# All low parts of the weights made on VectorE: 27 halves move from GpSimd's queue to VectorE's

## The chip, the cores and the metric

The kernel runs on one core of a Trainium2 chip. The metric is the device time of one execution in microseconds (us), taken as the median over the runs. Engines: TensorE (PE, with its weight loads PEld), VectorE (DVE), ScalarE (ACT), GpSimd (POOL), and SyncE (SP), which issues most of the DMA transfers.

## The reference

Two transformer blocks on 256 tokens of width 1024, in float32. The first block ends in a layer of product-key experts, and this is the part around the change:

```python
q = (hb @ w_query).reshape(t, PEER_HEADS, 2, PEER_HALF)
s = jnp.einsum('thpc,hpnc->thpn', q, sub_keys).astype(jnp.float32)
v1, i1 = lax.top_k(s[:, :, 0], PEER_TOPK)
v2, i2 = lax.top_k(s[:, :, 1], PEER_TOPK)
cand = (v1[..., :, None] + v2[..., None, :]).reshape(t, PEER_HEADS, PEER_TOPK * PEER_TOPK)
...
best, pos = lax.top_k(cand, PEER_TOPK)
experts = jnp.take_along_axis(cand_idx, pos, axis=-1)
gate = jax.nn.softmax(best, axis=-1).astype(hb.dtype)
...
act = jax.nn.gelu(jnp.einsum('thkd,td->thk', u, hb), approximate=False)
return jnp.einsum('thk,thkd->td', gate * act, vsel)
```

There are 8 heads with two key sets of 128 keys each, 16384 experts, and 16 chosen per head and token. Before it stand the modulation, retention and attention; behind it the second block's two gated feed-forward layers, a state-space mixer and a final projection.

## The kernel before

**Weights.** All weights come in chunks of 128 x 2048 float32 (1 MB) through three raw buffers (`NRAW`). A chunk is two halves of 128 x 1024. Half u belongs to chunk u // 2. Each half is split in two: ScalarE copies it to `w_hi` in the matmul's reduced float32 format (`ahead` in `scalar_program`, line 1608), and `w_lo` = raw - `w_hi` is made by VectorE (`ahead`, line 2118) or, for the halves in `LO_POOL` (line 131), by GpSimd (`ahead`, line 2893; its results are listed at line 2903). There are four buffers of each (`NH`), so the high part of a half waits until TensorE has used the half four before it. `ahead(u)` makes the parts up to half u+3 (`AHEAD`, `REACH`). TensorE computes a half of the expert layer in `feat_half` (line 1297): 16 products with the high part, then a wait for the low part, then 8 products with the low part; then it signals `s_used`. SP loads a chunk when both lows of the chunk three before it are made (line 902, `read`).

**Order.** Each engine's queue is written out by hand, in program order.

**Queries, halves 48 to 63** (`U_QUERY` = 48). For c = 0 to 7, TensorE computes halves 48+2c and 49+2c, then the key scores of c-1 (`key_scores`, line 1334); behind the last two halves it makes those of 6 and 7 one behind the other. ScalarE makes the high parts, copies the queries out of PSUM when both halves of c are used, and then the scores of c-1. VectorE (lines 2513 to 2519) makes lows up to 48+2c+4, waits for the scores of c, and takes the best 16 of four tables (`top16`: max, index, replace).

**Experts, halves 64 to 135 in this stretch** (`U_PEER` = 64). TensorE goes on with one half after another and ScalarE applies `gelu` to each pair. VectorE meanwhile chooses the experts, for each of two blocks of 128 tokens (line 2560): `candidates` adds the score pairs and takes the best 16 of 256 for 8 heads; `chosen(i, 0)` and `chosen(i, 1)` turn positions into indices; between them it reduces `gsel`, for which ScalarE first applies `Exp`. ScalarE does that `Exp` behind the `gelu` of chunk 5 (halves 74 and 75) and of chunk 12 (halves 88 and 89). Between these steps `keep_up` and `ahead` make low parts: up to 70 ahead of the first block's long `top16`, up to 75 behind it, up to 83 ahead of the second block's, up to 88 behind it, and up to 96 at the end. TensorE turns the choice behind half 93 (`turn_choice`), VectorE copies it and makes one-hot tables, and from there TensorE mixes one-hot products (`g_block`) with the halves.

**GpSimd** makes the lows of its 27 halves: 52 to 68, 71 to 75 and 84 to 88. Ahead of 71 and of 84 it waits until VectorE has made the low just before. Behind that it has only a few small instructions and transfers.

The lines of VectorE's queue around the queries:

```python
            for c in range(8):
                for m in range(2):
                    ahead(U_QUERY + 2 * c + m)
                v.wait_ge(s_kse, 2 * c + 2)
                top16([(v16[i][:, hp, :], ix[i][:, hp, :], Ss[i][:, hp, :])
                       for i in range(2) for hp in (2 * c, 2 * c + 1)])
```

Of the kernel before, what the change touches and what calls it, by code (L numbers as in the profile page):

```python
# [84 lines left out]
U_FRONT, U_OUT1, U_QUERY, U_PEER = 0, 40, 48, 64  # L85
# [37 lines left out]
def ffn_at(base, c):  # L123
# [4 lines left out]

LO_POOL = (set(range(U_QUERY + 4, U_PEER + 5)) | set(range(U_PEER + 7, U_PEER + 12))
           | set(range(U_PEER + 20, U_PEER + 25)))

# [272 lines left out]
def program(nc, wall, keys_d, cols_d, rows_d, bigrows_d, crow_d, wmod_d, dist_d, x_d, ctx_d, pT_d, gws_d, out_d, n_chunks):  # L408
    assert n_chunks * 2 == U_END
    with ExitStack() as es:  # L410
# [142 lines left out]
        def lows(u):  # L553
            pool = sum(1 for w in LO_POOL if w <= u)
            return (s_lop, pool) if u in LO_POOL else (s_lov, ORD[u] + 1 - pool)

# [1528 lines left out]
        def vector_program(e):  # L2085
# [32 lines left out]
            def ahead(u, only=False, late=0):  # L2118

                nonlocal made  # L2120
                while made < (ORD[u] + 1 if only else REACH[u] - late):
                    w = SPLIT[made]
                    if w not in LO_POOL:
                        v.wait_ge(s_hi, made + 1)
# [764 lines left out]
        def gpsimd_program(e):  # L2889
# [3 lines left out]
            def ahead(u):  # L2893

                nonlocal made
                while made < REACH[u]:
                    w = SPLIT[made]
                    if w in LO_POOL:
                        if w in (U_PEER + 7, U_PEER + 20):
# [156 lines left out]
```

How the kernel before makes its waits and increments, by code:

```python
    def wait_ge(self, sem, value):  # L58
        if self.passed.get(sem.name, 0) < value:
            self.passed[sem.name] = value
            self.e.wait_ge(sem, value)
# [1 line left out]
    def settle(self):  # L63
        if self.prev is not None:
            self.wait_ge(*self.prev)
# [800 lines left out]
        def sync_program(e):  # L867
# [2 lines left out]
                if n == 2:  # L870
                    e.dma_start(x[:, :, :], x_d.rearrange("(i p) d -> p i d", p=128)).then_inc(s_x, 16)
                    e.dma_start(crow, crow_d[0:1024].partition_broadcast(128)).then_inc(s_crow, 16)
                if n == 4:
                    e.dma_start(ctx, ctx_d.rearrange("(i p) d -> p i d", p=128)).then_inc(s_ctx, 16)
                if n == 1:
                    e.dma_start(rows[:, :], rows_d.partition_broadcast(128)).then_inc(s_rows, 16)
                if n == 10:
                    e.dma_start(dist, dist_d.rearrange("p (a b) -> p a b", a=4)).then_inc(s_tab, 16)
                if n == U_OUT1 // 2 - 1:
                    e.wait_ge(s_c2, 2)
                    e.dma_start(crow_keep.rearrange("(p d) -> p d", p=1), crow[0:1, :]).then_inc(s_ckeep, 16)
                if n == U_QUERY // 2:
                    e.wait_ge(s_pt_, 8)
                    e.dma_start(skeep, keys_d).then_inc(s_keys, 16)
                if n == U_QUERY // 2 + 4:
                    e.wait_ge(s_res, result(N_PEER, 1, 1))
                    e.dma_start(x_keep, x[:, :, :].rearrange("p i d -> p (i d)")).then_inc(s_xkeep, 16)
                if n == PEER_V[54] // 2:
```

## Time and profile before

| | |
|---|---|
| median of 3 runs | 1691.32 us (1691.31 to 1691.42) |
| profiled execution, its own time | 1691.32 us |
| its span, first to last instruction | 1689.3 us |
| mean granted TensorE clock | 0.989 |
| busy PE | 1629.5 us (96%) |
| busy DVE | 1270.1 us (75%) |
| busy ACT | 966.5 us (57%) |
| busy POOL | 72.7 us (4%) |
| low parts on DVE | 471, mean 1225 ns |
| low parts on POOL | 27, mean 2402 ns |

Times in the profile are counted from the first instruction of the span. An instruction's row has its start, its duration, its engine and line, what it writes and reads, and in brackets the idle time of its engine just before it and what ended that. Most operations are issued by small helpers, so many rows name a helper's line (2092 for VectorE's two-input operations, 1606 for all of ScalarE's, 930 for TensorE's products); what is written and read tells them apart. A row of several instructions has their count behind an x. The durations of products overlap, so the step from one row's start to the next is the better measure.

### The profile page before, as it was taken

What the parts mean: (1) busy time and instruction counts of PE and PEld (TensorE: products, weight loads), DVE (VectorE), ACT (ScalarE), POOL (GpSimd) and SP (SyncE); (2) the same over time, 40 slices, a digit from 0 to 9 for tenths busy, and PEclk for the clock granted to TensorE, in tenths of its full rate; (3) what the DMA queues carried; (4) which work ended last, traced back from release to release, by engine and by line L of the source; (5) the groups of instructions that cost most, each with busy time, mean ns of one, the idle gap of its engine ahead of it and who ended that gap; (6) DMA issues with size and microseconds to landing.
All of it is one profiled execution on the core that took longest, in us unless ns stands there. A gap on an engine that the chain in (4) does not pass through costs nothing.

```text
span 1689.3 us, 26937 instructions
## 1 busy us (share of the span) xinstructions
PE 1629.5 (96%) x10328; PEld 1394.9 (83%) x10328; DVE 1270.1 (75%) x2048; ACT 966.5 (57%) x1342; POOL 72.7 (4%) x46
## 2 busy tenths in 40 slices
PE   7999889998999999999999999999998989999997
PEld 2777679998999888888888888888888778888886
DVE  3668766999888999987777666776666887676666
ACT  5546655554555454555555555665556767665556
POOL 0000007520000000000000000000000000000000
PEclk9999899999999999999999999999999999999999
DMA  8644235356555455566655555455543533555551
GB/s 341 252 171 162 91 119 203 151 171 208 190 188 188 175 194 212 192 255 223 215 213 211 206 206 200 150 209 190 196 178 138 224 126 125 206 200 183 200 191 76
DMA packets 53266, 317.86 MB, mean 188 GB/s; under 512 B 5937, under 2 KB 6097, under 8 KB 19218
## 3 DMA queue, kind: packets, MB, share of 16 engines
q1 hardware_dynamic: 51954, 310.08, 50.4%
q0 software_dynamic: 1184, 6.05, 0.9%
q8 instruction: 82, 1.34, 0.3%
q14 instruction: 46, 0.38, 0.1%
HBM read 306.65 MB, written 9.47 MB: 187 GB/s over the span
## 4 chain that ended last, share of the span: by engine, by line
PE 79%; DVE 14%; ACT 4%; issue 1%; DMA 1%; SPq 0%; DVEq 0%; ACTq 0%
PE pb L930 79%; DVE w_lo L2092 4%; DVE ar L2092 3%; ACT ar L1606 2%; DVE ar L2104 2%; DVE ar L2506 1%; ACT w_hi L1606 1%; DVE ar L2503 1%; DMA raw<-in_wall 1%; ACT L1606 1%; DVE ar L2510 1%; DVE ar L2278 0%; DVE ar L2108 0%; DVE sm L2356 0%; PE pb L1245 0%
## 5 line engine op out<-in xcount | busy, mean ns | idle before, releaser
L2092 DVE TENSOR_TENSOR w_lo<-raw,w_hi 128x1024 fp32r<-128x1024 f32 x471 | 577.2, 1225 | 173.8 <-ACT w_hi L1606 142.5
L1606 ACT ACTIVATE w_hi<-raw 128x1024 fp32r<-128x1024 f32 x498 | 528.7, 1062 | 141.2 <-PE pb L930 97.8
L930 PE MATMUL pb<-HX,w_hi 128*128 128x256 f32 (+1 forms) x2768 | 509.2, 331 | 7.8 <-DVE ar L2092 3.3
L930 PEld LDWEIGHTS pb<-HX,w_hi 128*128 128x128 f32 x2768 | 415.3, 192 | 49.1 <-DVE ar L2092 3.6
L930 PE MATMUL pb<-w_hi,HC 128*128 128x512 f32 (+1 forms) x1648 | 446.5, 391 | 3.8 <-DVE HC L2104 2.1
L930 PEld LDWEIGHTS pb<-w_hi,HC 128*128 128x128 f32 x1648 | 302.0, 189 | 64.9 <-issue 4.9
L1606 ACT ACTIVATE ar<-pb 128x256 f32<-128x256 f32 (+2 forms) x320 | 152.6, 477 | 322.8 <-PE pb L930 220.0
L2092 DVE TENSOR_TENSOR ar<-ar 128x512 bf16<-128x512 bf16 (+9 forms) x506 | 268.6, 566 | 43.4 <-ACT ar L1606 19.8
L930 PE MATMUL pb<-HX,w_lo 128*128 128x256 f32 x1952 | 279.1, 284 | 2.5 <-DVE w_lo L2092 2.2
L930 PEld LDWEIGHTS pb<-HX,w_lo 128*128 128x128 f32 x1952 | 263.8, 192 | 14.6 <-DVE w_lo L2092 3.3
L930 PE MATMUL pb<-w_lo,HC 128*128 128x512 f32 (+1 forms) x824 | 255.4, 388 | 0.0
L930 PEld LDWEIGHTS pb<-w_lo,HC 128*128 128x128 f32 x824 | 154.4, 188 | 32.5
L930 PE MATMUL pb<-w_hi,HX 128*128 128x512 f32 x512 | 142.1, 399 | 2.9 <-ACT w_hi L1606 2.0
L930 PE MATMUL pb<-ar 128*128 128x64 bf16 (+3 forms) x1960 | 125.2, 223 | 10.9 <-issue 3.6
L930 PEld LDWEIGHTS pb<-ar 128*128 128x128 bf16 (+2 forms) x1960 | 105.2, 120 | 33.1 <-issue 22.1
L930 PEld LDWEIGHTS pb<-w_hi,HX 128*128 128x128 f32 x512 | 93.7, 189 | 23.3 <-ACT w_hi L1606 3.1
L1606 ACT ACTIVATE HC<-ar 128x512 fp32r<-128x512 f32 (+1 forms) x89 | 55.4, 623 | 83.1 <-PE pb L930 46.9
L1606 ACT ACTIVATE ar<-ar 128x512 f32<-128x512 f32 (+7 forms) x108 | 66.1, 612 | 56.9 <-DVE ar L2092 32.8
L2092 DVE TENSOR_TENSOR ar<-pb,ar 128x512 f32<-128x512 f32 (+1 forms) x87 | 58.6, 673 | 49.4 <-ACT ar L1606 42.7
L2092 DVE TENSOR_TENSOR HC<-ar,HC 128x512 fp32r<-128x512 f32 (+1 forms) x89 | 60.5, 680 | 32.5 <-ACT HC L1606 27.8
L930 PE MATMUL pb<-w_lo,HX 128*128 128x512 f32 x256 | 79.7, 392 | 0.5 <-DVE w_lo L2092 0.3
L2903 POOL TENSOR_TENSOR w_lo<-raw,w_hi 128x1024 fp32r<-128x1024 f32 x27 | 64.9, 2402 | 102.8 <-ACT w_hi L1606 62.0
(148 smaller groups left out, 673.2 us busy)
## 6 DMA issues: line engine op xcount, KB each, us to landing
raw<-in_wall SPq DMA_DIRECT2D x257, 1024.0 KB, 4.9
ar<-in_wmod SPq DMA_DIRECT2D x24, 512.0 KB, 3.9
act_keep<-ar SPq DMA_DIRECT2D x28, 256.0 KB, 5.6
ar<-act_keep SPq DMA_DIRECT2D x28, 256.0 KB, 5.1
x<-in_wmod SPq DMA_DIRECT2D x8, 512.0 KB, 5.5
ar<-in_bigrows POOLq DMA_DIRECT2D x2, 1024.0 KB, 4.8
ar<-acs_keep POOLq DMA_DIRECT2D x2, 1024.0 KB, 7.9
x<-in_x SPq DMA_DIRECT2D x1, 1024.0 KB, 11.4
```

What stands on the lines that cost most here:

```text
L930: return e.matmul(o, l, r, start=start, stop=stop, skip_group_check=True)
L1606: a.did(e.activation(out, in_, func, scale=scale, **kw), sig)
L2092: v.did(e.tensor_tensor(out, a_, b_, op), sig)
L2104: v.did(e.scalar_tensor_tensor(out, a_, s_, b_, op0, op1), sig)
L2503: v.did(e.max(vals[:, c_], src))
L2506: v.did(e.max_index(idx[:, c_], vals[:, c_], src))
L2510: v.did(e.match_replace(src, vals[:, c_], src, NEG))
L2903: p.did(e.tensor_tensor(w_lo[:, made % NH, :], raw_half(w), w_hi[:, made % NH, :].bitcast(F32), SUB), s_lop)
```

## The change

The set `LO_POOL` becomes empty. The low parts of its 27 halves are then made by VectorE, in the places of its queue where its `ahead` passes them, and TensorE and SP wait for VectorE's count `s_lov` where they waited for GpSimd's `s_lop`. GpSimd's `ahead` makes nothing. Nothing else is different.

```diff
-LO_POOL = (set(range(U_QUERY + 4, U_PEER + 5)) | set(range(U_PEER + 7, U_PEER + 12))
-           | set(range(U_PEER + 20, U_PEER + 25)))
+LO_POOL = set()
```

## Rows read from the trace of the kernel before

**Rows 1.** Windows: length; busy PE, PEld, DVE, ACT, POOL (count); clock; DMA

```profile
261.43:301.30 39.87, 39.87 (x338) 39.87 (x337) 31.06 (x192) 20.92 (x30) 28.79 (x12) 1.00 0.43 159
301.30:358.69 57.39, 57.11 (x473) 56.61 (x472) 54.83 (x177) 31.54 (x35) 16.86 (x7) 1.00 0.41 154
358.69:401.67 42.98, 37.18 (x304) 36.34 (x304) 40.74 (x106) 19.80 (x22) 12.03 (x5) 0.98 0.63 209
401.67:560.00 158.33, 158.33 (x1896) 154.60 (x1897) 136.81 (x234) 82.08 (x103) 0.00 (x0) 0.98 0.56 184
```

**Rows 2.** Chain of waits, 240 to 450: start, us, what; between these VectorE throughout

```profile
246.42 54.03 PE pb L930 x440
...
399.41 1.04 DVE ar L2092 x2
```

**Rows 3.** Low parts, 250 to 402: duration ns min/median/max; and three of VectorE's

```profile
L2903 POOL TENSOR_TENSOR w_lo<-raw,w_hi x27: 2374/2407/2417, 252.3 to 369.3; 128x1024 fp32r<-128x1024 f32 x27
L2092 DVE TENSOR_TENSOR w_lo<-raw,w_hi x19: 1224/1225/1226, 250.0 to 394.5; 128x1024 fp32r<-128x1024 f32 x19
...
391.81 3.88 DVE L2092 TENSOR_TENSOR w_lo<-raw,w_hi 128x1024 fp32r<-128x1024 f32 x3
```

**Rows 4.** Timeline of TensorE in the queries: key scores of two turns

```profile
266.15 1.05 PE L930 MATMUL pb<-ar 128*128 128x128 f32 x8
...
272.80 1.05 PE L930 MATMUL pb<-ar 128*128 128x128 f32 x8
```

**Rows 5.** Timeline of VectorE in the queries: first and second top16

```profile
261.43 0.68 DVE L2503 MAX8 ar<-ar 128x8 f32<-128x128 f32 x3 [10.17 <-ACT ar L1606]
...
268.07 0.87 DVE L2503 MAX8 ar<-ar 128x8 f32<-128x128 f32 x4 [1.33 <-ACT ar L1606]
...
273.10 0.28 DVE L2506 FIND_INDEX8 ar<-ar 128x8 uint32<-128x128 f32 x1
```

**Rows 6.** Timeline of TensorE: products behind two pauses

```profile
377.51 1.21 PE L930 MATMUL pb<-HX,w_lo 128*128 128x256 f32 x8 [1.26 <-DVE w_lo L2092]
378.56 2.08 PE L930 MATMUL pb<-HX,w_hi 128*128 128x256 f32 x16
...
401.67 1.44 PE L930 MATMUL pb<-ar 128*128 128x64 bf16 x24 [3.62 <-issue]
402.91 3.76 PE L930 MATMUL pb<-HX,w_hi 128*128 128x256 f32 x16
```

**Rows 7.** Timeline of VectorE: candidates, choice and copy

```profile
318.00 2.71 DVE L2503 MAX8 ar<-ar 128x8 f32<-128x256 f32 x8
...
333.36 0.29 DVE L2092 TENSOR_TENSOR ar<-ar 128x128 f32<-128x128 f32 x1
...
342.62 0.29 DVE L2112 TENSOR_REDUCE sm<-ar 128x8 f32<-128x128 f32 x1
...
358.69 2.71 DVE L2503 MAX8 ar<-ar 128x8 f32<-128x256 f32 x8
...
374.05 0.29 DVE L2092 TENSOR_TENSOR ar<-ar 128x128 f32<-128x128 f32 x1
...
383.32 0.28 DVE L2112 TENSOR_REDUCE sm<-ar 128x8 f32<-128x128 f32 x1
...
395.79 1.22 DVE L2108 COPY ar<-pb 128x384 f32<-128x384 f32 x2
```

**Rows 8.** TensorE: a window of 1 us (length, busy, clock, DMA); a later pause

```profile
406.00:407.00 1.00, 1.00 (x7) 0.58 1.14 131
...
1302.98 2.55 PE L930 MATMUL pb<-HX,w_hi 128*128 128x256 f32 x16 [3.27 <-DVE ar L2092]
```

**Rows 9.** Timeline of ScalarE: gelu of chunk 5, then Exp

```profile
335.97 0.60 ACT L1606 ACTIVATE x<-pb 128x512 f32<-128x512 f32 x1 [1.77 <-PE pb L930]
...
337.94 0.31 ACT L1606 ACTIVATE ar<-ar 128x128 f32<-128x128 f32 x1
```

**Rows 10.** DMA issues of the page: KB each, median us to landing

```profile
raw<-in_wall SPq DMA_DIRECT2D x257, 1024.0 KB, 4.9
```

## The prediction

> **What bounds the kernel now.** I read the busy shares first: TensorE is busy nearly all the time, GpSimd hardly at all, so only the stretch in which GpSimd works can matter. The table of stretches [rows 1] splits it. From 261.43 to 301.30 (the queries) TensorE has no idle time and VectorE is busy 31.06 of 39.87 us. From 301.30 to 401.67 (candidates and choice) VectorE is busy 54.83 + 40.74 = 95.57 of 100.37 us. From 401.67 to 560 TensorE has no idle time again. The chain of waits [rows 2] says the same: TensorE until 300.45, then VectorE's own queue, instruction behind instruction, with short gaps until 400.45, and TensorE's one-hot products from 401.67. So VectorE is the bound for 100 us, and it has room only in the queries. None of the 27 GpSimd instructions is on the chain.
>
> **The price of one low part.** GpSimd takes 2.40 us, VectorE 1.23 us [rows 3]. Three in a row take 391.81 to 395.79 [rows 3, 7], so a further one costs 1.32.
>
> **Part 1, the queries (halves 52 to 64).** One turn of line 2513's loop is 6.65 us: TensorE starts key scores at 266.15 and the next turn's at 272.80 [rows 4]; a half is 2.88. ScalarE copies the scores, VectorE's `top16` starts at 268.07 and ends at 273.38, 5.31 us; VectorE idles 1.33 us in each turn [rows 5]. If VectorE's room alone counted, two lows (2.65) against 1.33 of idle would cost 1.3 us a turn. But order counts: in turn c VectorE first makes the lows of halves 48+2c+3 and 48+2c+4 and only then waits for the scores of c; TensorE makes those scores behind half 48+2c+3. The low of that half now stands behind `top16` of c-1 and ahead of the scores, which gives a round trip that nothing covers: `top16` 5.31, 0.1, low 1.23, 0.05 to TensorE, 1.05 for its eight low products after a pause (377.51 to 378.56 [rows 6]), 1.92 from the start of key scores to `top16` (266.15 to 268.07). Sum 9.66 against 6.65: 3.0 us a turn. The other low (1.32) is hidden in the 2.97 us after the first. The first low, of half 52, falls in the 10.17 us of idle before 261.43 [rows 5] and is free. From the first `top16` to the seventh there are six such turns: 18.0 us. The eighth needs no further half (keys 6 and 7 are made one behind the other), so it is late by its two lows, 2.6 more. Halves 67 and 68, just behind it, add 2.6. **Subtotal 23.2 us** at the first `top16` of `candidates`, 318.00 before.
>
> **Part 2, the bursts (halves 71 to 75 and 84 to 88).** `top16` of the candidates is 15.3 us long (318.00 to 333.36, 358.69 to 374.05 [rows 7]) and makes no low part; GpSimd made five meanwhile. TensorE can run only to half 70 and through the high products of 71. The low of 70 comes just ahead of `top16`, TensorE has about 4.3 us of work left at its start, and the low of 71 ends 16.9 us after it: some 12 us of pause. In the second round its backlog is about 2 us more, so some 10. VectorE then makes five in a burst: 5 x 1.32 = 6.6 us each round, 13.2 together.
>
> TensorE starts again late and, after such a pause, at the low clock. Behind the pause of 3.62 us at 401.67 sixteen high products are listed with 3.76 us where 2.08 is their length at full clock, so they ran at 1.2 GHz [rows 6]. The window from 406 to 407 has a clock of 0.58, so 2.4 GHz came back at about 406.8 [rows 8]. Those 5.1 us at half speed are at most 2.6 us of excess, the sixteen products alone are 1.7; I take 2.2. Call T the end of the burst's first low. Then:
> - Round one. Half 73 is used at T+8.9; ScalarE copies `gelu` (0.6) and makes the high part of 77 (1.06) by T+10.7; VectorE wanted it at T+9.7 (4 x 1.32, then 1.85 and 2.59 of the choice's steps between the lows). Half 75 is used at T+0.96+4x2.88+2.2 = T+14.7. Only behind it does ScalarE take `gelu`, a table load and the `Exp` that VectorE's reduction needs: `gelu` starts at 335.97, 0.2 us behind TensorE, and the `Exp` ends at 338.25, 2.48 us in all [rows 9], so T+17.2. Before, this lay 4.4 us ahead of the reduction at 342.62 [rows 7]. VectorE comes to it at T+15.2 and waits 2.0. From there to the next `top16` is 16.07 us (342.62 to 358.69), so T+33.3. With 1.63 us from the end of `top16` to T that is 34.9 against 25.33 before: +9.6.
> - Round two. The `Exp` stands behind half 89, the sixth of the burst: T+0.96+5x2.88+2.2+2.48 = T+20.1, while VectorE comes at T+14.9. It waits 5.2. From the reduction to the copy of the choice is 12.47 us (383.32 to 395.79): T+32.6, with 1.63 that is 34.2 against 21.74: +12.5.
>
> Both contain the 6.6 of lows; waits are 3.0 and 5.9.
>
> **What covers, and what is late next.** The copy at 395.79 becomes 441.1, and the one-hot products, 5.88 us later, 447.0. Halves 94 and 95 fill TensorE between, and TensorE's last pause is 2.7 us instead of 3.62. Behind it TensorE had no idle time to 560 [rows 1] and its order is fixed, so nothing is given back. SP reloads a raw buffer only when both lows are made, and is late with VectorE; a load lands 4.9 us after issue [rows 10], and a burst's next load, issued at T, is wanted at T+6, when half 72 has been used, so I cost it at nothing; if it is not hidden, 1 us a round. GpSimd's queue holds nothing else before its row of gates, which waits for `s_av` and `s_gcp` of earlier work.
>
> **Sum.** 18.0 + 2.6 + 2.6 + 9.6 + 12.5 = 45.3 us. The profiled execution took 1691.32 (span 1689.3), the same as the median, so 1736.6. Two unknowns of the clock pull on it. The new pauses in the queries are 2.97 us, once a turn. The trace has slow products behind 3.27 us [rows 8] and full-speed ones behind 1.26 [rows 6]; 2.97 lies between, nearer to the former. If the clock falls, lows and keys take up to 1.8 us more in that turn; TensorE's slower work then eats the next pause, so at most each second turn seems likely: 0 to 5.4, hard limit 11. Below, if the clock stays up behind the 2.7 us pause at the end, 2.2 us of excess go. I take both at nothing, since they are of one size and opposite sign, and round down: **1736 us**. The likeliest case's own range is 1730 to 1742.
>
> **Rivals.**
> - *Room, not order (8%).* The lows only lengthen VectorE's queue: 6 x 1.3 in the queries, 2.6 + 2.6 + 13.2 after, no waits on `Exp` or high parts: 26 us, 1718. For it: VectorE's idle before each `top16` is real. Against: the order of lines 2513 to 2519 and the window of four buffers.
> - *The clock falls in the query pauses (17%).* The same round trip at 1.2 GHz: +5 to +11 on the forecast, 1742 to 1748.
> - *Faster (2%).* A low by GpSimd takes 1.17 us longer than by VectorE. If TensorE were waiting for GpSimd's lows, the change would give back up to 27 x 1.17 = 31.6 us, 1660. It decides where TensorE's idle time ends on a GpSimd low. No row shows one: TensorE has no idle time in the queries, and its longest wait for a low, 1.26 us at 377.51, ends on VectorE's [rows 6]. The Trainium skill (GPSIMD Engine Reference, Engine selection) says to put elementwise work on VectorE since GpSimd is about 2x slower with two inputs; 2402 against 1225 ns agrees with its ratio, but the ratio says nothing about which queue is full here. By that rule alone the change would win the 31.6 us. The same page (Specifications) says that GpSimd contends with VectorE's two-input instructions for SBUF; by that rule the change would also quicken such instructions, but the low on VectorE has one duration throughout, 1224 to 1226 ns [rows 3].
> - *No effect (1%).* The lows would have to be hidden wholly, or the set be read elsewhere. The three places that read `LO_POOL` follow it, and 100 us of full VectorE queue speak against hiding.
>
> **Chances.** Forecast 72%, rivals as above. Range: low end, forecast without the waits for `Exp` and high parts (8.9) and without the last clock drop (2.2): 1725.5; high end, the clock's hard limit: 1747.6. So 1725 to 1748. A measurement of this kernel can tell about 0.2% (3.4 us) from no change. Faster 2%, within 1%, slower 97%.
>
> **What would show it.** In the profile after: 498 lows on VectorE and none on GpSimd; `top16` in the queries about 9.7 us apart; TensorE pauses there of about 3 us that end on VectorE's low; TensorE pauses of 12 and 10 us in the bursts; VectorE waiting about 2 and 5 us for ScalarE's `Exp` ahead of its reductions; the one-hot products from about 447; the rest shifted and unchanged. Query turns of 8 us would make part 1 wrong; idle TensorE under 8 us in a burst, part 2; granted clock 0.5 in the query pauses gives the second rival.

## The result, and the profile after

The changed kernel takes 1741.78 us (median of 4, 1741.23 to 1742.12), against 1691.37 for the one before in the same runs: ratio 1.0295, interval [1.0282, 1.0308], 50.4 us slower. The forecast was 1736 in a range of 1725 to 1748. The profiled execution's span is 1740.2 us, 50.9 more.

The page's rows of the busy shares and of the low parts; VectorE has all 498, GpSimd none, and TensorE has a new wait, 39.8 us ahead of its low products. It was 2.5 us before (the last row, from the page of the kernel before):

```profile
PE 1641.2 (94%) x10328; PEld 1405.6 (81%) x10328; DVE 1303.0 (75%) x2075; ACT 966.5 (56%) x1342; POOL 7.7 (0%) x19
...
L2091 DVE TENSOR_TENSOR w_lo<-raw,w_hi 128x1024 fp32r<-128x1024 f32 x498 | 610.2, 1225 | 178.9 <-ACT w_hi L1605 144.7
...
L929 PE MATMUL pb<-HX,w_lo 128*128 128x256 f32 x1952 | 284.5, 287 | 39.8 <-DVE w_lo L2091 39.8
...
L930 PE MATMUL pb<-HX,w_lo 128*128 128x256 f32 x1952 | 279.1, 284 | 2.5 <-DVE w_lo L2092 2.2
```

VectorE's timeline, first instruction of `top16` in the queries; these rows answer [rows 5] (line numbers of the kernel are one lower than before):

```profile
263.40 0.87 DVE L2502 MAX8 ar<-ar 128x8 f32<-128x128 f32 x4 [8.00 <-ACT ar L1605]
...
268.81 2.56 DVE L2091 TENSOR_TENSOR w_lo<-raw,w_hi 128x1024 fp32r<-128x1024 f32 x2
274.38 0.87 DVE L2502 MAX8 ar<-ar 128x8 f32<-128x128 f32 x4 [3.01 <-ACT ar L1605]
...
284.06 0.87 DVE L2502 MAX8 ar<-ar 128x8 f32<-128x128 f32 x4 [1.70 <-ACT ar L1605]
...
295.40 0.87 DVE L2502 MAX8 ar<-ar 128x8 f32<-128x128 f32 x4 [3.38 <-ACT ar L1605]
...
305.07 0.87 DVE L2502 MAX8 ar<-ar 128x8 f32<-128x128 f32 x4 [1.70 <-ACT ar L1605]
...
314.74 0.87 DVE L2502 MAX8 ar<-ar 128x8 f32<-128x128 f32 x4 [1.70 <-ACT ar L1605]
...
326.09 0.87 DVE L2502 MAX8 ar<-ar 128x8 f32<-128x128 f32 x4 [3.38 <-ACT ar L1605]
...
334.17 0.88 DVE L2502 MAX8 ar<-ar 128x8 f32<-128x128 f32 x4
```

A turn that was 6.65 us is 10.98, 9.68, 11.34, 9.67, 9.67 and 11.35 long. VectorE still sits idle in each turn, behind two lows: neither engine is full, the round trip between them is the bound. TensorE's timeline shows the other side:

```profile
270.10 2.07 PE L929 MATMUL pb<-HX,w_lo 128*128 128x256 f32 x8 [2.77 <-DVE w_lo L2091]
...
281.08 1.21 PE L929 MATMUL pb<-HX,w_lo 128*128 128x256 f32 x8 [2.79 <-DVE w_lo L2091]
...
365.13 2.08 PE L929 MATMUL pb<-HX,w_lo 128*128 128x256 f32 x8 [11.00 <-DVE w_lo L2091]
...
414.81 2.07 PE L929 MATMUL pb<-HX,w_lo 128*128 128x256 f32 x8 [10.49 <-DVE w_lo L2091]
...
453.32 1.03 PE L929 MATMUL pb<-ar 128*128 128x64 bf16 x24 [2.80 <-issue]
```

Eight low products are listed with 1.21 us at the full clock and with 2.07 at half of it. The first two rows have the same pause ahead of them and different clocks. VectorE's rows of candidates, choice and copy answer [rows 7]:

```profile
348.10 2.71 DVE L2502 MAX8 ar<-ar 128x8 f32<-128x256 f32 x8
...
363.86 6.54 DVE L2091 TENSOR_TENSOR w_lo<-raw,w_hi 128x1024 fp32r<-128x1024 f32 x5
...
375.36 1.23 DVE L2091 TENSOR_TENSOR w_lo<-raw,w_hi 128x1024 fp32r<-128x1024 f32 x1 [0.59 <-ACT w_hi L1605]
...
381.71 0.29 DVE L2111 TENSOR_REDUCE sm<-ar 128x8 f32<-128x128 f32 x1 [1.96 <-ACT ar L1605]
...
397.78 2.71 DVE L2502 MAX8 ar<-ar 128x8 f32<-128x256 f32 x8
...
434.95 0.29 DVE L2111 TENSOR_REDUCE sm<-ar 128x8 f32<-128x128 f32 x1 [5.12 <-ACT ar L1605]
...
447.44 1.22 DVE L2107 COPY ar<-pb 128x384 f32<-128x384 f32 x2
```

**Where 50.9 us went**, stretch by stretch, after against before:

| stretch, by VectorE's marks | before | after | more | forecast |
|---|---|---|---|---|
| start to first `top16` of the queries | 261.43 | 263.40 | 2.0 | 0 |
| first to seventh `top16` | 39.87 | 62.69 | 22.8 | 18.0 |
| seventh to `top16` of the candidates | 16.70 | 22.01 | 5.3 | 5.2 |
| round one | 40.69 | 49.68 | 9.0 | 9.6 |
| round two, to the copy | 37.10 | 49.66 | 12.6 | 12.5 |
| copy to one-hot products | 5.88 | 5.88 | 0 | 0 |
| one-hot products to the end | 1287.63 | 1286.88 | -0.8 | 0 |

### The profile page after: what moved, and what is told of

It is laid out like the page before. It is cut to its first block, busy times and chain, and to the rows that moved or that the text cites. A ratio compares the mean times of both kernels' runs of the same rounds, so it can differ in the third digit from the quotient of the medians.

```text
span 1740.2 us, 26937 instructions
## 1 busy us (share of the span) xinstructions
PE 1641.2 (94%) x10328; PEld 1405.6 (81%) x10328; DVE 1303.0 (75%) x2075; ACT 966.5 (56%) x1342; POOL 7.7 (0%) x19
## 4 chain that ended last, share of the span: by engine, by line
PE 78%; DVE 14%; ACT 5%; issue 1%; DMA 1%; SPq 0%; DVEq 0%; ACTq 0%
PE pb L929 77%; DVE w_lo L2091 4%; ACT ar L1605 2%; DVE ar L2091 2%; DVE ar L2505 2%; DVE ar L2103 2%; DVE ar L2502 1%; ACT w_hi L1605 1%; DVE ar L2509 1%; ACT L1605 1%; DMA raw<-in_wall 1%; DVE ar L2277 0%; DVE sm L2355 0%; PE pb L1244 0%; DVE ar L2096 0%
## 5 line engine op out<-in xcount | busy, mean ns | idle before, releaser
L2091 DVE TENSOR_TENSOR w_lo<-raw,w_hi 128x1024 fp32r<-128x1024 f32 x498 | 610.2, 1225 | 178.9 <-ACT w_hi L1605 144.7
L929 PEld LDWEIGHTS pb<-HX,w_hi 128*128 128x128 f32 x2768 | 420.8, 195 | 49.0 <-DVE ar L2091 3.8
L929 PE MATMUL pb<-HX,w_lo 128*128 128x256 f32 x1952 | 284.5, 287 | 39.8 <-DVE w_lo L2091 39.8
L929 PEld LDWEIGHTS pb<-HX,w_lo 128*128 128x128 f32 x1952 | 268.0, 195 | 53.0 <-DVE w_lo L2091 41.9
L929 PEld LDWEIGHTS pb<-ar 128*128 128x128 bf16 (+2 forms) x1960 | 105.7, 121 | 31.6 <-issue 21.1
L929 PEld LDWEIGHTS pb<-w_lo,HX 128*128 128x128 f32 x256 | 47.9, 189 | 13.2 <-DVE w_lo L2091 2.9
```

What stands on the lines that cost most here:

```text
L929: return e.matmul(o, l, r, start=start, stop=stop, skip_group_check=True)
L2091: v.did(e.tensor_tensor(out, a_, b_, op), sig)
```

## Experiments

The theory is the forecast's: what counts is not how many lows VectorE gets but where each stands in the round between two engines. Its rival is that only VectorE's room counts. Times of each experiment are compared with the kernel before on the same chip, by ratio; its median there was 1692.5, 1691.7 or 1692.7. Where an experiment is set against the changed kernel, that is its 1741.78 from the first runs; as the medians of the kernel before differ by 1.3 us between the sets of runs, such differences are good to about 1 us, and the rows say more.

**1. The queries alone**, from the kernel before.

```diff
-LO_POOL = (set(range(U_QUERY + 4, U_PEER + 5)) | ...
+LO_POOL = (set(range(U_QUERY + 17, U_PEER + 5)) | ...
```

> The kernel before with only the lows of halves 52 to 64 moved to VectorE; 65 to 68 and both bursts stay on GpSimd. Order theory (a low stands between top16 of one turn and the scores of the next): six turns of 9.66 us or more instead of 6.65, +18.0, and +1.3 to 1.7 in each turn in which the clock falls as it did three times in the changed kernel, +4.7: 1709 to 1716, near 1714. Room theory (only VectorE's idle time counts): turns of 8.0, +8: 1699.

1713.98 us, ratio 1.0134 [1.0117, 1.0151], or 22.7 us by the ratio. Its turns are 9.67, 10.96, 9.67, 11.36, 9.66 and 10.16 long. The order theory's number, not the room theory's 1699.

**2. The bursts alone**, from the kernel before.

```diff
-LO_POOL = (set(range(U_QUERY + 4, U_PEER + 5)) | set(range(U_PEER + 7, U_PEER + 12))
-           | set(range(U_PEER + 20, U_PEER + 25)))
+LO_POOL = set(range(U_QUERY + 4, U_PEER + 5))
```

> The kernel before with only the bursts moved to VectorE (halves 71 to 75 and 84 to 88); 52 to 68 stay on GpSimd. If the second part of the sum stands by itself: +9.0 and +12.5 as in the changed kernel, of which 13.2 are the lows and the rest waits of VectorE for high parts and for the Exp: 1712 to 1713, with waits of about 2 and 5 us ahead of the two reductions. If only room counts: +13.2, 1704.6, and no such waits.

1712.61 us, ratio 1.0125 [1.0108, 1.0142], 21.2 us. The waits view of VectorE from 300 to 460 has the `Exp` in its first row (total, times, longest):

```profile
DVE sm L2111 <- ACT ar L1605: 7.1, 2, 5.1
DVE w_lo L2091 <- ACT w_hi L1605: 1.5, 2, 0.8
```

So the second part stands by itself: 22.7 + 21.2 and the 5.3 of halves 65 to 68, which neither moves, make 49.2 of the 50.4.

**3 and 4. Same number of lows, other place.** From the kernel before, one low alone in each turn goes to VectorE: in the third experiment that of the odd half, which TensorE needs ahead of the next scores, in the fourth that of the even half, which it needs behind them.

The added lines end, in the third experiment (53, 55 ... 63 to VectorE) and then in the fourth (54, 56 ... 64):

```diff
+            | set(range(U_PEER + 20, U_PEER + 25))) - set(range(U_QUERY + 5, U_PEER, 2)))
...
+            | set(range(U_PEER + 20, U_PEER + 25))) - set(range(U_QUERY + 6, U_PEER + 1, 2)))
```

> The kernel before with the lows of the odd halves 53, 55 to 63 alone moved to VectorE, one in each turn of the queries. Order theory: each of them is the low ahead of the next scores, so the round trip is as long as with two: turns of 9.66, +18.0, and +1.3 to 1.7 for each fall of the clock: 1709 to 1716. Room theory: one low of 1.32 us fits the idle 1.33 of a turn: 1691 to 1692.

1717.66 us, ratio 1.0149 [1.0132, 1.0166].

> The kernel before with the lows of the even halves 54, 56 to 64 alone moved to VectorE: as many instructions of the same length as with the odd ones, in the same place of VectorE's queue, but TensorE needs each of them only behind the scores for which VectorE waits next. Order theory: hidden, turns stay at 6.65: 1691 to 1692. Room theory: 1691 to 1692 as well. If any low added to VectorE here cost its length, +8: 1699.

1692.9 us, ratio 1.0003 [0.9994, 1.0013]. Six instructions of 1.23 us cost 25 us in one place and, in the other, nothing that the times can tell. That settles order against room. In the fourth experiment the low stands where VectorE was idle, and `top16` follows at once:

```profile
264.68 0.87 DVE L2503 MAX8 ar<-ar 128x8 f32<-128x128 f32 x4
266.84 1.23 DVE L2092 TENSOR_TENSOR w_lo<-raw,w_hi 128x1024 fp32r<-128x1024 f32 x1
268.17 0.87 DVE L2503 MAX8 ar<-ar 128x8 f32<-128x128 f32 x4
```

It fits only just. Five of its six turns are 6.74 or 6.75 us long instead of 6.65 and one is 7.09, so the seventh `top16` and the copy stand 0.9 us later than before.

The third missed its range by 1.7 us upward. Its turns are 9.70, 11.38, 12.06, 11.30, 9.68 and 11.81 long. Four are long by the clock instead of three, though each has one low less. And in two of these VectorE's low itself was slow, beside a low of GpSimd:

```profile
288.24 2.35 POOL L2903 TENSOR_TENSOR w_lo<-raw,w_hi 128x1024 fp32r<-128x1024 f32 x1 [10.11 <-ACT w_hi L1606]
289.33 2.33 DVE L2092 TENSOR_TENSOR w_lo<-raw,w_hi 128x1024 fp32r<-128x1024 f32 x1
```

This low took 2.33 us instead of 1.23, that of the sixth turn 1.69: 1.6 us together, which puts the turns of 12.06 and 11.81 above the longest of the changed kernel. The sixth turn of the first experiment, 10.16, has the same cause: its two lows took 3.02 us instead of 2.56.

**5. The Exp earlier**, in the changed kernel.

```diff
-                    if c in (5, 12):
-                        a.wait_ge(s_gs, 1 if c == 5 else 2)
+                    if c in (4, 10):
+                        a.wait_ge(s_gs, 1 if c == 4 else 2)
```

> The changed kernel, with ScalarE's Exp placed behind the gelu of chunk 4 (halves 72 and 73) and of chunk 10 (84 and 85) instead of 5 and 12. If VectorE's waits of 1.96 and 5.12 us ahead of its reductions end on the Exp that stands too late in ScalarE's order: both go to about nothing; TensorE's halves then are the next thing late, so the gain is 2 to 7 us: 1735 to 1740, the second round's pause gone most. If these waits are set by something else (the high parts), nothing changes: 1741.8.

1736.68 us, 5.1 less than the changed kernel's median. Not all of it is the edit's. In the profiled executions the spans differ by 5.2 us: 0.9 of it stands ahead of the first `top16`, which the edit doesn't reach, 2.9 between there and the copy, and 1.4 behind the copy, where the clock stayed up this time (the 24 one-hot products are listed with 0.90 us instead of 1.03). The two waits of 7.1 us ahead of the reductions are gone from VectorE's waits; those for high parts in the bursts rise instead, from 1.6 (0.59 + 0.99) to 5.4 us. The Exp did set these waits, and behind it TensorE's backlog comes next.

**6 and 7. The long turns: is it the clock?** In the changed kernel, TensorE makes further products into an unused bank in the pause ahead of the low of each odd half: eight (0.96 us) in the sixth experiment, then twenty (2.4 us) in the seventh, whose edit is shown.

```diff
+                    if u in range(U_QUERY + 5, U_PEER, 2):
+                        for n in range(20):
+                            mm(PB[0][:, 0:256], hi[:, n % 8, :], HX[:, 0, n % 8, :], True, True)
                     t.wait_ge(*LOW[u])
```

> The changed kernel, and TensorE makes eight further products of 128 x 256 into an unused PSUM bank ahead of its wait for the low in halves 53, 55 to 63: 0.96 us of work in each pause of 2.8 us, which becomes 1.8. If the falls of the clock in three of the six turns cost 4.7 us: the clock stays up, all turns are 9.66, the time is 1737. If the long turns come from something else, the time stays at 1741.8 or rises.

1741.1 us (1739.1 to 1741.9): a miss. Two of its six turns were still long (11.22 and 11.07), behind pauses of 1.8 us. By this alone it stayed open whether the clock was the cause.

> The changed kernel with twenty further products of TensorE (2.4 us) in each pause of 2.8 us of the queries instead of eight. With eight, two turns of six were still 1.4 and 1.5 us too long. If falls of the clock make the long turns: with a pause of 0.4 us none falls, all turns are 9.67 and 4.7 us go: 1737. If the length of turns has another cause: 1741.

1736.57 us, 5.2 less than the changed kernel. All turns are 9.67 or 9.68, the pauses 0.37 or 0.38:

```profile
311.11 0.87 DVE L2505 MAX8 ar<-ar 128x8 f32<-128x128 f32 x4 [1.70 <-ACT ar L1608]
...
320.79 0.87 DVE L2505 MAX8 ar<-ar 128x8 f32<-128x128 f32 x4 [1.70 <-ACT ar L1608]
```

TensorE does 14 us more work and the kernel is 5 us faster. The six turns take 58.06 us against 62.69: 4.6 us of the 22.8 was the clock, 18.2 the round trip.

**8. The low in the middle of top16**, in the changed kernel: VectorE makes the next odd half's low between the two halves of `top16` instead of behind it.

```diff
-            def top16(jobs):
+            def top16(jobs, between=None):
                 for half_ in range(2):
+                    if half_ == 1 and between is not None:
+                        between()
...
+                      lambda: ahead(U_QUERY + 2 * c + 2) if c < 7 else None)
```

> The changed kernel with all lows on VectorE, but in the queries the low ahead of the next scores is made in the middle of the top16 before it. Order theory: the round trip is no longer the bound, VectorE's room is: 5.31 + 2.65 and two gaps, turns of 8.0 us, pauses of TensorE near 1.3 us and no fall of the clock: -10 for the order and -4.7 for the clock, 1727. If the lows cost what they cost wherever they stand: 1741.8.

1727.14 us, 14.6 less than the changed kernel, with the same instructions on the same engine. Turns are 8.07 to 8.08 us, VectorE is without a pause, TensorE's pauses there are 1.2 us (0.7 the first) and all its products of the queries run at full clock:

```profile
262.12 0.87 DVE L2504 MAX8 ar<-ar 128x8 f32<-128x128 f32 x4 [7.99 <-ACT ar L1605]
...
270.19 0.87 DVE L2504 MAX8 ar<-ar 128x8 f32<-128x128 f32 x4
```

Here room is the bound of a turn.

**9. Everything on GpSimd**, from the kernel before: all lows from 52 to 96, and no waits ahead of 71 and 84.

```diff
+LO_POOL = set(range(U_QUERY + 4, U_PEER + 33))
...
-                        if w in (U_PEER + 7, U_PEER + 20):
-                            p.wait_ge(*LOW[w - 1])
```

> The kernel before with the lows of all halves 52 to 96 on GpSimd (18 more), without GpSimd's waits ahead of 71 and 84. If VectorE's queue is the bound from 301 to 401: it is 22 us shorter there, TensorE's 94.3 us of work become the bound, the one-hot products start about 7 us earlier and the clock does not fall ahead of them (2.2): 1682 to 1686. If GpSimd's 2.40 us a low is too slow for TensorE's 2.88 a half, TensorE waits on GpSimd's lows: 1691 or more.

1715.65 us, ratio 1.0139 [1.0122, 1.0156]: 24 us slower where some 8 us faster was expected. The second theory's range holds the number, but not by its mechanism: TensorE never waits for a GpSimd low. VectorE's own instructions became long beside GpSimd's. The additions of the first block's candidates met four of its lows, and from 344.11 on it made 14 lows without a break (timelines of both engines):

```profile
315.29 11.63 DVE L2091 TENSOR_TENSOR ar<-ar 128x256 f32<-128x256 f32 x8
...
344.11 38.66 POOL L2900 TENSOR_TENSOR w_lo<-raw,w_hi 128x1024 fp32r<-128x1024 f32 x14 [5.72 <-ACT w_hi L1605]
```

VectorE's groups from 340 to 381, shapes apart (count, busy, mean ns), in this kernel:

```profile
L2091 DVE TENSOR_TENSOR ar<-ar 128x2048 bf16<-128x2048 bf16 x4 | 11.2, 2794 | 0.1
L2091 DVE TENSOR_TENSOR ar<-ar 128x1024 bf16<-128x1024 bf16 x2 | 5.6, 2784 | 0.1
L2091 DVE TENSOR_TENSOR ar<-ar 128x512 bf16<-128x512 bf16 x2 | 5.0, 2513 | 0.1
L2091 DVE TENSOR_TENSOR ar<-ar 128x128 f32<-128x128 bf16 x2 | 5.0, 2510 | 0.1
...
L2505 DVE FIND_INDEX8 ar<-ar 128x8 uint32<-128x256 f32 x6 | 2.4, 416 | 0.0
```

and the same shapes in the kernel before, from 332 to 352:

```profile
L2092 DVE TENSOR_TENSOR ar<-ar 128x2048 bf16<-128x2048 bf16 x4 | 4.9, 1225 | 0.1
L2506 DVE FIND_INDEX8 ar<-ar 128x8 uint32<-128x256 f32 x4 | 1.6, 419 | 0.0
L2092 DVE TENSOR_TENSOR ar<-ar 128x1024 bf16<-128x1024 bf16 x2 | 1.4, 691 | 0.1
L2092 DVE TENSOR_TENSOR ar<-ar 128x512 bf16<-128x512 bf16 x2 | 0.8, 424 | 0.1
...
L2092 DVE TENSOR_TENSOR ar<-ar 128x128 f32<-128x128 bf16 x2 | 0.6, 293 | 0.1
```

The two-input instructions on bf16 take 2.1 to 2.2 us longer each, most of one GpSimd low, whether their own work is 0.29 or 0.69 us. The largest do so too: of the four of 128x2048 the first began before GpSimd's lows and took 1.23 us, the other three took 3.31 or 3.32. The index search of one input keeps its 0.42. The eight additions of 128x256 take 11.63 us instead of 2.77. So the choice came late, and ScalarE, which had run ahead with TensorE, stood at its wait for the second `Exp`; the chain from there to TensorE:

```profile
401.98 0.31 ACT L1605 ACTIVATE ar<-ar 128x128 f32<-128x128 f32 x1 [22.64 <-DVE ar L2091]
...
403.43 3.78 PE L929 MATMUL pb<-HX,w_hi 128*128 128x256 f32 x16 [17.45 <-ACT w_hi L1605]
```

**10 to 12. Less on VectorE where it is the bound**, from the kernel before: a sixth low on GpSimd beside each `top16` of the candidates, where VectorE's instructions keep their durations; and the last of three lows ahead of the copy made later.

```diff
-LO_POOL = (set(range(U_QUERY + 4, U_PEER + 5)) | set(range(U_PEER + 7, U_PEER + 12))
-           | set(range(U_PEER + 20, U_PEER + 25)))
+LO_POOL = (set(range(U_QUERY + 4, U_PEER + 5)) | set(range(U_PEER + 7, U_PEER + 13))
+           | set(range(U_PEER + 20, U_PEER + 26)))
...
-            ahead(U_PEER + 2 * NU - NG - 1)
+            ahead(U_PEER + 2 * NU - NG - 1, late=1)
```

> The kernel before with one low more in each burst on GpSimd (halves 76 and 89), so that six lows of 2.4 us stand beside a top16 of 15.3 us, where VectorE's instructions have one input and were not slowed. If VectorE's queue is the bound there and the six fit beside top16: 2 x 1.3 us less, 1689. If the sixth runs into VectorE's two-input steps of the choice, which took twice their time beside GpSimd with all lows on it: the gain is eaten, 1691 to 1693.

1688.9 us, ratio 0.9981 [0.9972, 0.999].

> The kernel before with the last of three lows ahead of the copy of the choice (half 96) made behind the first one-hot tables instead, with the low of 97. If VectorE's queue sets the start of the one-hot products: they start 1.3 us earlier, 1690. If TensorE or the low of 96 is the next thing late: 1691.3.

1689.67 us, ratio 0.9986 [0.9977, 0.9995].

> Both edits in one kernel. If they add: 2.6 + 1.3 us less than before, 1687.5. If the sixth low of a burst costs what it gives: 1690.

1688.26 us, ratio 0.9972 [0.9961, 0.9983]: 4.7 us less by the ratio, faster than both kernels, and near the sum of the two. It is the opposite of the change: two lows more on GpSimd, placed by what VectorE does beside them. The one-hot products begin at 399.03, 400.21 and 399.69 instead of 401.67; the last execution was already 1.9 us late at `top16` of the candidates. Behind that point the three take 0.5, 0.8 and 1.0 us less than the kernel before: the mean granted clock from 400 to 405 was 0.66, 0.67 and 1.00 instead of 0.50. So a part of the gain is the clock's and not the queue's.

## Why the prediction was right, point by point

- **What bounds.** Right. The fourth experiment shows how narrow the room was: one low a turn, 1.32 us with its gap, fills the 1.33 us of idle, and the seventh `top16` was 0.9 us late. The last three experiments gain by what they take from VectorE's queue.
- **Part 1, order.** Right in mechanism and size: 9.67 us for a turn at full clock, 9.66 worked out. The two lows more ahead of the eighth `top16` and halves 67 and 68 took 2.66 and 2.65 against 2.6 each.
- **The clock in the queries.** The mechanism stood in the sum at nothing and among the rivals with +5 to +11; it was 4.6 us. The step that was mis-sized is "I take both at nothing, since they are of one size and opposite sign". Of the 2.2 us that should offset it only 0.8 came: the clock fell behind the last pause too, of 2.80 us, and one window of 1 us there shows it (length, busy, clock, DMA):

```profile
456.00:457.00 1.00, 1.00 (x7) 0.50 0.00 0
```

  The 4.6 us, the 2.0 us of which a point below tells, less these 0.8, are nearly all of the 5.6 us between the sum of 45.3 and the 50.9 of the trace. The median, 1741.78, lies at the upper end of the likeliest case's own range (1742), where the clock rival begins. The whole range had room for it because its upper end was worked out from this same mechanism.

- **"At most each second turn."** That held: turns one, three and six are long, and none follows another. In the third experiment three in a row were long, so it is no rule.
- **Part 2, bursts.** Right: 9.0 and 12.6 against 9.6 and 12.5. The pauses are 11.00 and 10.49 (12 and 10 forecast), the waits for the `Exp` 1.96 and 5.12 (2.0 and 5.2). Round one is 0.6 too long in the sum because its low clock cost less: from 365.13 the low products and the next high ones took 1.6 us more than at full clock, not 2.2.
- **Nothing given back behind 401.67.** Right, to 0.8 us, and these are the clock's: from the start of the one-hot products at 453.32 the lag behind the kernel before falls from 51.65 to 50.9 us over the first 6 us and stays there to the end. The low clock lasted less long than before.
- **2.0 us ahead of the first moved instruction.** Not in the sum. The first low that the change moves is made at 254.18; TensorE's products at 233.57 before stand at 235.46 already. The change can't reach there. The mean clock of the first 40 us was 0.96 in this execution and 1.00 before, and the twelfth experiment's kernel shows a shift of the same size. That kernel still has its lows on GpSimd, so the shift is how two executions differ; why the clock differs there stays open. About 49 of the 50.9 us are then the change's, as the 22.7, 21.2 and 5.3 above also say.
- **The 2x of GpSimd.** The rival that the change could win 27 x 1.17 = 31.6 us was rightly given 2%. On contention the forecast said that the low on VectorE has one duration throughout. That row was true, but it couldn't show what was asked: in the kernel before GpSimd's 27 lows ran beside `top16` or beside nothing, so no two-input instruction was ever beside one. The first, third and ninth experiments put them there. What the Trainium skill says (GPSIMD Engine Reference, Specifications), that the two contend where VectorE's instruction has two SBUF inputs, agrees with it. It would not have changed this forecast.

## What to carry to other kernels

When work moves to an engine with idle time, follow each instruction in program order to who needs it next; if the engine then waits for an answer to that very instruction, its place costs the whole round trip, and moving it by half a loop body can win most of that back (14.6 us here). An Exp or a table load placed "late enough" in a third engine's order is part of the deal as well: it was slack before and a wait of 5 us after. Before using GpSimd as a helper, look at what VectorE runs beside it.

## What the runs showed of the hardware

- In the ninth experiment VectorE's two-input instructions on bf16 beside a stream of GpSimd's two-input ones took 2.1 to 2.2 us longer each, whatever their size (2.4 to 3.3 us where it is 0.29 to 1.23 alone). In the third, one low met one low and took 2.33 us instead of 1.23. Max, index search and replacement did not change. Of the others, one cast of 128x512 took 2.10 instead of 0.43, one copy of 128x384 2.58 instead of 0.36. GpSimd's own longest low was 3.2 us instead of 2.4.
- The length of a pause does not tell whether TensorE's clock falls. Behind 2.77 to 2.79 us it fell three times and stayed up twice in one execution; behind the last pause of the queries, 3.25 us in the first experiment, eight low products took 1.22 us, and behind 3.24 us in the third 2.07. With pauses of 1.8 us it fell in two turns of six; with 0.38 never. Twenty unused products in each pause were cheaper than the pauses, by 5.2 us; eight were not enough (1741.1).
